# Storing the residual stream block by block, and summing the norm's squares on TensorE

## What is computed

```python
for i in range(DEPTH):                        # DEPTH = 2, D_MODEL = 1024, D_FF = 2816
    m = mixer(rmsnorm(x, norm_mix_g[i]), ...) # z = h @ w_in; three causal mixers; concat @ w_o
    x = x + m
    gate, up = split(rmsnorm(x, norm_ffn_g[i]) @ w_ffn_in[i], 2)
    x = x + (silu(gate) * up) @ w_ffn_out[i]
return rmsnorm(x, norm_final_g)
```

## Time and profile before

| What | Value |
|---|---|
| median of 3 runs | 1450.1 us (1449.74 to 1450.79) |
| the profiled execution | 1450.79 us, its slowest core's span 1449.7 us |
| spans of the 8 cores | 1437.2 to 1449.7 us |
| mean granted TensorE clock | 0.984 to 0.991 of full speed |
| TensorE busy | 95% of the span |
| VectorE, ScalarE busy | 46%, 27% |
| chain that ended last | 85% of it TensorE |

### The profile page before, as it was taken

The page is one execution under the profiler, slowest core; times in us unless marked ns, Lnnn a source line. Parts: engine busy times, 40 slices in busy tenths (PEclk is TensorE's granted clock), DMA queues, the critical chain, the costliest instruction groups (busy, mean ns, idle before and its releaser), DMA issues.

```text
span 1449.7 us, 23400 instructions; the slowest of 8 cores (1437.2 to 1449.7 us)
## 1 busy us (share of the span) xinstructions
PE 1371.4 (95%) x8038; PEld 785.3 (54%) x8148; DVE 671.1 (46%) x1323; ACT 394.5 (27%) x754; POOL 80.6 (6%) x156
## 2 busy tenths in 40 slices
PE   3879899899999999999998999999999999999996
PEld 1446554555555555555465755465555555555544
DVE  2556869842222322223783686994222332222378
ACT  3435544421110011112332454442111001111232
POOL 0001100000000000000000210000000000000000
PEclk8989999999999999999999999999999999999998
DMA  9835461313122312212154646130312222222114
GB/s 204 203 70 100 89 149 30 59 16 59 31 41 39 52 22 40 50 21 36 53 126 72 102 87 153 30 59 6 68 22 40 35 40 44 45 45 36 21 59 176
DMA packets 51107, 95.27 MB, mean 66 GB/s; under 512 B 6256, under 2 KB 26256, under 8 KB 50960
## 3 DMA queue, kind: packets, MB, share of 16 engines
q0 software_dynamic: 16704, 56.63, 23.4%
q1 hardware_dynamic: 34288, 37.14, 9.2%
HBM read 132.22 MB, written 13.33 MB: 100 GB/s over the span
## 4 chain that ended last, share of the span: by engine, by line
PE 85%; DVE 6%; DMA 3%; issue 3%; ACT 2%; SPq 0%; POOL 0%; DVEq 0%; ACTq 0%; POOLq 0%
PE ps L540 85%; DMA xT<-x_in 2%; DVE hT L527 2%; DMA poly<-hist 1%; DVE xT L524 1%; ACT shr L516 1%; SPq L224 0%; DVE xT L527 0%; DVE shr L527 0%; DVE shr L524 0%; DVE sum_50 L524 0%; DVE sum_92 L524 0%; ACT shr L509 0%; DVE hist L524 0%; DVEq L379 0%
## 5 line engine op out<-in xcount | busy, mean ns | idle before, releaser
L540 PE MATMUL ps<-hT,ring 128*128 128x512 bf16 (+3 forms) x5095 | 919.2, 337 | 9.3 <-DVE shr L527 2.7
L540 PEld LDWEIGHTS ps<-hT,ring 128*128 128x128 bf16 x5168 | 505.5, 98 | 400.4 <-issue 11.8
L540 PE MATMUL ps<-gT,ring 128*128 128x512 bf16 (+2 forms) x1732 | 306.8, 337 | 1.6
L540 PEld LDWEIGHTS ps<-gT,ring 128*128 128x128 bf16 x1760 | 172.4, 98 | 134.7
L524 DVE TENSOR_TENSOR xT<-ps,xT 128x512 f32<-128x512 f32 (+2 forms) x240 | 138.6, 584 | 133.2 <-PE ps L540 131.5
L516 ACT ACTIVATE shr<-xT 128x512 f32<-128x512 f32 (+5 forms) x186 | 99.5, 554 | 153.7 <-DVE xT L524 128.5
L527 DVE SCALAR_TENSOR_TENSOR hT<-xT,pD,shr 128x512 bf16<-128x512 f32 (+2 forms) x120 | 69.6, 640 | 7.8 <-ACT shr L509 7.8
L509 ACT ACTIVATE fs_56<-ps 128x512 f32<-128x512 f32 (+2 forms) x37 | 19.0, 513 | 157.9 <-PE ps L540 147.1
L509 ACT ACTIVATE fs_98<-ps 128x512 f32<-128x512 f32 (+2 forms) x37 | 19.0, 513 | 157.9 <-PE ps L540 147.0
L524 DVE TENSOR_TENSOR gT<-ps,fs_56 128x512 bf16<-128x512 f32 (+2 forms) x37 | 21.7, 587 | 77.6 <-PE ps L540 77.6
L524 DVE TENSOR_TENSOR gT<-ps,fs_98 128x512 bf16<-128x512 f32 (+2 forms) x37 | 21.7, 587 | 77.3 <-PE ps L540 77.3
(11 more groups left out here) (225 smaller groups left out, 802.0 us busy)
## 6 DMA issues: line engine op xcount, KB each, us to landing
ring<-w_fi POOLq DMA_DIRECT2D x44, 512.0 KB, 5.3
ring<-w_fo POOLq DMA_DIRECT2D x32, 352.0 KB, 4.5
ring<-w_in POOLq DMA_DIRECT2D x18, 512.0 KB, 7.2
ring<-w_tp POOLq DMA_DIRECT2D x12, 640.0 KB, 7.6
xT<-x_in SPq DMA_DIRECT2D x6, 1024.0 KB, 22.3
y_out<-xT SPq DMA_DIRECT2D x6, 1024.0 KB, 4.7
ring<-w_o POOLq DMA_DIRECT2D x8, 512.0 KB, 5.8
poly<-hist SPq DMA_DIRECT2D x48, 64.0 KB, 4.6
```

Of the source, the lines that this page charges most:

```text
L540: k.node("pe", [((lambda e, p=p: e.matmul(ap(p[0]), lhsT=p[1], rhs=p[2], start=p[3], stop=p[4])), max(width(p[0]), 40) * 0.43, p[5] if len ...
```

## The change

`xT`, `x_in` and `y_out` are stored block by block: all 8 chunks of block 0, then of block 1, and so on. Four chunks of a block are one run of 8 KB (4 KB in blocks 3 and 4). `v32` now covers blocks 2 and 3 (`VB`) wholly, and only these are saved to `xscr` and reloaded, in two transfers. The blocks are gone through in the order `OB = [0, 1, 4, 2, 3]` in `unit_g`, the output projection, `ffn` and all of layer 1's mixer. `sq_one` always writes bf16 and issues one ones-matmul for each chunk; the fp32 sums are gone. `TAIL` is 3, and in that tail all eight `sq_one` of a block stand behind its last `unit_out`. The due time of an output transfer counts from its own place in the program, no longer from its end.

```diff
+VB = (2, 3)
+V0, V1 = 8 * BL[2][0], 8 * (BL[3][0] + BL[3][1])
+OB = [0, 1, 4, 2, 3]
...
-                d = nd.T + 60000.0 if nd.late is None else self.clock + nd.late
+                d = nd.T + (60000.0 if nd.late is None else nd.late)
...
+        def X(m, b, k_=1):
+            c0, n = BL[b][0], BL[b][1]
+            return xT[:, 8 * c0 + m * n:8 * c0 + (m + k_) * n]
...
-                k.dma("sp", xT[:, 4 * hh:4 * hh + 4, c0:c0 + n], x_in[:, 4 * hh:4 * hh + 4, c0:c0 + n],
+                k.dma("sp", X(4 * hh, b, 4), xd(x_in, 4 * hh, b, 4),
...
+        def sq_one(b, m):
             c0, n = BL[b][0], BL[b][1]
+            si = cnt["sq"] % NSQ
+            cnt["sq"] += 1
+            square(sqt[si][:, 0:n], X(m, b), [b_x[m][b]], [b_sqt[si]])
             if b not in stat:
...
-            square(sq32[si][:, 0:n], xv, [b_x[m][b]], bs)
-            if i < 7:
-                tt(acc, acc, sq32[si][:, 0:n], ALU.add, bs + [bacc], [bacc])
...
+            mm(pi[:, 0:n], [(ones_b[:], sqt[si][:, 0:n])], [b_sqt[si], b_const], pi, i == 0, i == 7)
...
-            v32 = xT[:, 5:8, :].rearrange("p k t -> p (k t)")[:, 0:NG * NN].rearrange("p (g n) -> p g n", g=NG)
+            v32 = xT[:, V0:V1].rearrange("p (g n) -> p g n", g=NG)
...
-                for b in range(5):
+                for b in VB:
...
-            for b in range(5):
+            for b in OB:
...
-            TAIL = 6
+            TAIL = 3
...
-                    for b in range(5):
-                        for m in range(8 - TAIL, 8):
-                            unit_out(g, m, b)
-                            sq_one(b, m, sums=sums)
+                    for b in OB:
+                        for m in range(8):
+                            if m >= 8 - TAIL:
+                                unit_out(g, m, b)
+                            sq_one(b, m)
...
-        mixer(1, [0, 1, 2, 3, 4])
+        mixer(1, OB)
```

More of the change, by code:

```diff
@@ L497, in build_program @@
         shr = sb(st, "shr", [128, 2560], F32)
+        NSQ = 4
+        sqt = [shr[:, 1024 + 256 * i:1280 + 256 * i].bitcast(BF16) for i in range(NSQ)]
+        b_sqt = k.bufs(NSQ)
         nrs = [shr[:, 512 * i:512 * i + 512] for i in range(2)]
[L499 to L503, removed]
+        b_nrs = k.bufs(2)
         b_pAB, b_pPP, b_pC, b_pD, b_Wm, b_bias2 = k.bufs(6)
@@ L1043, in mixer @@
             for g in range(NG // 2):
-                k.alias([B[("v", g)]], [b_x[m][b] for m in range(5, 8) for b in range(5)])
-            k.alias([B[(n_, i)] for n_ in ("cb", "vb", "vs") for i in range(3)], b_norm)
+                k.alias([B[("v", g)]], [b_x[m][b] for m in range(8) for b in VB])
+            k.alias([B[(n_, i)] for n_ in ("cb", "vb", "vs") for i in range(3)], b_sqt + b_nrs)
             conv = deque(range(NG // 2))
@@ L1078, in mixer @@
             sample_silu()
-            k.alias(b_norm, [B[(n_, i)] for n_ in ("cb", "vb", "vs") for i in range(3)])
-            for b in range(5):
+            k.alias(b_sqt + b_nrs, [B[(n_, i)] for n_ in ("cb", "vb", "vs") for i in range(3)])
+            for b in OB:
                 c0, n = BL[b][0], BL[b][1]
@@ L1105, in mixer @@
                         norm(b, 2 + l)
-                    if b == 4 and m % 2:
+                    if b == OB[4] and m % 2:
                         ring.done(("o", l, m // 2))
@@ L1114, in ffn @@
             NF = 3
-            sums = [(sb(sf, "sum%d" % i, [128, 512], F32), k.buf()) for i in range(5)]
             fs = [sb(sf, "fs%d" % i, [128, 512], F32) for i in range(NF)]
@@ L1158, in ffn @@
                 for m in range(8 - TAIL if last else 8):
-                    for b in range(5):
+                    for b in OB:
                         unit_out(g, m, b)
-                        if last:
-                            sq_one(b, m, sums=sums)
                     ring.done(("fo", l, g, m))
                 if last:
-                    for b in range(5):
-                        for m in range(8 - TAIL, 8):
-                            unit_out(g, m, b)
-                            sq_one(b, m, sums=sums)
+                    for b in OB:
+                        for m in range(8):
+                            if m >= 8 - TAIL:
+                                unit_out(g, m, b)
+                            sq_one(b, m)
                         norm(b, 4 if l == 1 else 1)
-                        if l == 0:
+                        if l == 0 and b in VB:
                             c0, n = BL[b][0], BL[b][1]
-                            k.dma("sp", xscr[:, :, c0:c0 + n], xT[:, 5:8, c0:c0 + n], reads=[b_x[m][b] for m in range(5, 8)],
-                                  writes=[b_xscr])
+                            k.dma("sp", xscr[:, 8 * c0 - V0:8 * (c0 + n) - V0], X(0, b, 8), reads=[b_x[m][b] for m in range(8)],
+                                  writes=[b_xscr[b]])
                     for m in range(8 - TAIL, 8):
@@ L1177, in ffn @@
                 k.retire(r_)
-            k.retire(b_fs + [b_ for _, b_ in sums])
+            k.retire(b_fs)
             sf.close()
-        b_xscr = k.buf()
+        b_xscr = dict(zip(VB, k.bufs(2)))
         mixer(0, border0)
         ffn(0)
-        mixer(1, [0, 1, 2, 3, 4])
+        mixer(1, OB)
         ffn(1)
@@ L1257, in by_time @@
         return y[:, :, :SEQ].reshape(128, 8, 16, R, CI).transpose(2, 4, 3, 1, 0).reshape(SEQ, D)
+    for o in out:
+        o["y_out"] = np.concatenate([o["y_out"][:, 8 * c0:8 * (c0 + n)].reshape(128, 8, n) for c0, n, _, _ in BL], axis=2)
     y_prompt = np.stack([by_time(o["y_out"]) for o in out])
```

76 lines of the change are left out of this document (30 added, 46 removed).

## The result

The changed kernel takes 1460.05 us (median of four executions) against 1449.92 us before: ratio 1.0067, 95% interval 1.0047 to 1.0086. So it is 0.7% slower; the forecast was +5.8 us, the result about +10.

A forecast was written before the change was run, and what follows sets the result against it. TensorE, busy 95% of the span, was taken as the bound; less VectorE work pays only in the output projections. 24.4 - 9 - 6 - 4 + 0.4 = +5.8 us gave 1456 us, range 1447 to 1463 us.

The forecast's parts named there:

- the load of `x`: Kernel start: longer packets land block 0 earlier, so steady matmuls begin 6 us sooner; ends 0 and 11 us.
- the start of the convolution: Layer 1, A's convolution: other matmuls cover the `poly` wait, 6.8 us in all; 2.8 left for `vtok`, so -4 us.
- The ones-matmuls, +24.4 us: Output projection and `ffn`, both layers: 140 more ones-matmuls on TensorE, 6.1 us in each of four places.
- The adds of squares, -9 us: Output projections: dropping VectorE's adds removes 9 of 10.9 us of stalls and half clock; nothing gained in `ffn`.
- rival 2: Added ones-matmuls wait for squares or their buffers, some 1.2 us a place, +5 us in all: 1461 us; chance 9%.
- the one from 81 to 47 ns a KB: Load of blocks 3 and 4: long early packets reach the later rate, taking 6.2 instead of 10.4 us, 4.2 us less.
- the step from the landing to the matmuls: Kernel start: order stays the same, so what block 0 lands earlier shifts everything behind it, steady matmuls included.
- The end, +0.4 us: After the last `unit_out`: 11.3 us to the last multiply instead of 9.7, less 1.2 already counted with the ones-matmuls.
- An edit at nothing: Save and reload of `x`: same bytes in fewer transfers, no TensorE wait for the reload, so priced at 0.
- a cover for the reload: `unit_g`: VectorE is still busy there when the reload lands, and block 2 now comes fourth, so no wait.

The follow-up runs named there:

- the run with the sums everywhere: Changed kernel's layout, block order and reload, but fp32 sums of squares on VectorE, one ones-matmul a block and `TAIL = 6`; 1451.02 us, ratio 1.0028 to the kernel before.

## Why the prediction came out as it did

The sign and the range held: 1460 us lies in 1447 to 1463, but just above the forecast's own 1453 to 1459. Three of the terms did what was said of them. Two gains were too large, and both err to the same side: the load of `x`, where two steps of the reasoning failed, and the start of the convolution, which was priced on one core.

**The ones-matmuls, +24.4 us: right.** 0.215 us each, without a wait in front. In `ffn`, where nothing hides them, they cost 6.08 us in layer 0 and 5.29 + 0.27 us in layer 1 (6.1 and 6.1 + 0.4 forecast), and putting the fp32 sums back took exactly that away. A part of it belongs to `TAIL = 3`: with `TAIL = 6` and the same ones-matmuls the last `ffn` with the kernel's end is 3.2 us shorter.

**The adds of squares, -9 us: right.** The output projections with what lies around them changed by -1.28 + 4.30 - 1.44 = +1.6 us and -1.41 + 2.69 - 0.61 = +0.7 us. With 6.1 us of ones-matmuls in each, the stalls given back are 4.5 and 5.4, together 9.9 us. Some of that is the layout's: between the run with the sums everywhere and the change, which share it, the same stretches differ by 2.2 and 1.5 us, so the squares alone give back about 8.5. VectorE is 62 us less busy, not 80: 15 squares moved there from ScalarE, among other things. The bank or square wait of rival 2 is absent: 0.6 us in each place.

**The load of `x`, -6 us: too large.** It measured -2.6 us as a mean of the cores. Two steps failed. The first is the one from 81 to 47 ns a KB: the early packets were to reach the late rate once they were long. SP's queue in the changed kernel, 3 to 8 us, then 24 to 30 us:

```profile
q1 hardware_dynamic: 253, 0.91, 79.1%
...
q1 hardware_dynamic: 266, 1.93, 100.5%
```

0.791 x 16 x 5 us / 253 = 250 ns for a packet of 3.6 KB, 70 ns a KB early on; 1.005 x 16 x 6 us / 266 = 363 ns for 7.3 KB, 50 ns a KB later. Length took the early rate from 81 to 70, not to 47. Blocks 3 and 4 thus gain, as an estimate, 2.1 MB x 11 ns a KB / 16, 1.4 us, where 4.2 were forecast; the second half of block 4 landed 1.2 us earlier (23.8 to 22.6 us as a mean). What holds the early rate down was not tested.

The second is the step from the landing to the matmuls: what block 0 lands earlier was to shift everything behind it. Block 0's second half did land 5.0 us earlier (34.0 to 29.0 us as a mean), but then it no longer ended last. Before, ScalarE waited for it on six of the eight cores, 1.0 to 2.9 us (on core 2 the wait of 1.94 us in the earlier trace rows). With the change no core waits for it. ScalarE's timeline on core 6, then VectorE's:

```profile
23.50 1.07 ACT L527 ACTIVATE shr<-xT 128x272 bf16<-128x272 f32 x3 [4.00 <-DMA xT<-x_in]
...
28.50 3.40 ACT L527 ACTIVATE shr<-xT 128x512 bf16<-128x512 f32 x6
```

```profile
28.69 3.39 DVE L538 SCALAR_TENSOR_TENSOR hT<-xT,pD,shr 128x272 bf16<-128x272 f32 x8 [1.90 <-ACT shr L520]
32.00 1.29 DVE L528 TENSOR_TENSOR shr<-xT 128x512 bf16<-128x512 f32 x2
36.21 5.39 DVE L538 SCALAR_TENSOR_TENSOR hT<-xT,pD,shr 128x512 bf16<-128x512 f32 x8 [2.93 <-ACT shr L520]
```

The squares of block 0 (512 columns) stand behind the norm of block 4 (272 columns), whose second half ScalarE had waited for until 23.50 us. So block 4's chain now ends last, and block 0's first multiply comes only 2.5 us earlier (38.6 to 36.1 us as a mean).

Against the Trainium skill's "DMA: Bandwidth & Descriptors" (Specifications: line rate from 512 B), 1 KB and 2 KB runs were slower here than 4 KB and 8 KB ones, 185 to 199 and 283 to 329 GB/s where only the runs differ. The Trainium skill's "Perfetto Trace Analysis" (DMA Optimizations) speaks of the size of a whole DMA: small ones, under 2 KB, carry an overhead, and batching 2 KB into 4 or 8 KB can help much. Here each DMA moved 0.5 to 1 MB in either kernel and only the runs inside it grew; the trace shows 8 and 16%, the same sign.

A further slip is in the choice of the core: core 2, the slowest before, began its steady matmuls at 48.32 us, 2.6 us behind the mean of the eight. Its gain (to 43.17 us on the slowest core after) looks like the forecast, but part of it is that core's chance, and it was gone after the `poly` wait of layer 0, which took 8.60 us instead of 6.31 on the slowest core: there the lead was 107.77 - 104.55 = 3.2 us.

**The convolution in layer 1, -4 us: too large, read on one core.** It measured -1.2 us as a mean. The wait for `poly` went as forecast and one for `vtok` came (2.85 us on every core; 2.8 had been set aside). But before the change only five of the eight cores waited for `poly` there, 3.3 to 4.7 us, core 2 among them. On cores 3, 5 and 7 TensorE already waited for `vtok`; core 5:

```profile
787.94 0.41 PE L540 MATMUL ps<-WmT,vtok_66 128*64 128x128 bf16 x8 [2.74 <-DVE vtok_66 L535]
```

Up to the end of C's work the five cores gain 2.4 us as a mean (core 2 64.9 to 61.7, so 3.2 of its 4), and the three lose 0.7. The half clock behind `vtok`, which the forecast left out, came on core 6 alone: 3.59 us for eight matmuls that take 1.73 at full clock and about 0.6 us more in the five behind them. There this stage takes 63.4 us, on each of the others 61.7.

**The end, +0.4 us: +0.27.** The sum with the measured terms: 24.4 - 9.9 - 2.6 - 1.2 = +10.7, with +0.2 of `unit_a`, -0.3 of layer 0 before `unit_b` and some 0.6 us less in layer 1's `ffn` with the end, +10.0 us, which the table has as +9.94.

**An edit at nothing that had a price.** The saves were called "the same bytes in fewer transfers". They are 3 MB that start when the next layer's weights are due, and only `TAIL = 3` kept that from costing what the run with `TAIL = 6` shows, 10.8 us in layer 1 and 7 in all. The price was hidden, not absent, and the prediction named a cover for the reload but none for the saves.

## What to carry to other kernels

Work moved off an engine pays only in the stages in which that engine ends last, here two stretches of some 85 us each out of 1450. There, three of the eight squares sent to TensorE, and none in `ffn`, already took the stalls away, at less than half of the price. When a transfer that ended last is made faster, look for the chain that will end last next; here half of the gain went to it. When transfers are merged, look at what else the queue's engines move at the moment when the merged one starts. And read a wait on all cores before it is priced.

## What the runs showed of the hardware that was not expected

Packets four times as long raised the early rate of a load on eight cores from 185 to 199 GB/s a core only, but the rate 20 us later from 283 to 329. A stall of 2.85 us on TensorE was followed, on core 6, by a granted clock of 0.50, the lower of its two levels, for the 2 us from 802 us and the 2 us after:

```profile
802.00:804.00 2.00, 2.00 (x6) 0.76 (x5) 1.72 (x6) 0.00 (x0) 0.88 (x2) 0.50 1.06 245
804.00:806.00 2.00, 2.00 (x8) 0.90 (x6) 0.85 (x3) 0.60 (x1) 0.00 (x0) 0.50 0.55 80
```

On the other seven cores the same stall, at the same place of the list, left it at 1.00; core 0, where the stall ends at 800.39 us:

```profile
800.00:802.00 2.00, 1.61 (x14) 0.89 (x15) 1.69 (x7) 0.00 (x0) 0.16 (x1) 1.00 1.03 270
802.00:804.00 2.00, 1.19 (x8) 0.59 (x6) 1.71 (x6) 0.60 (x1) 0.72 (x2) 1.00 1.02 209
```

So the length of a stall did not decide it; what did was not tested. The 0.6 us stalls in the output projections left the clock at 1.00 too.
